# The last expert's rows go to their tokens by one-hot fp32 products, the other experts' rows are summed during its down products

## The chip, the core and the metric

The kernel runs on one core of one Trainium2 chip, alone. The metric is the device time of one execution in microseconds (us), the smaller the better. TensorE does the matrix products (PE in the rows, PEld its weight loads), VectorE (DVE) and ScalarE (ACT) the elementwise work and the reading of PSUM, GpSimd (POOL) some elementwise work and all indirect DMAs, SyncE (SP) issues the large weight loads.

## The reference, cut to what matters

Two layers (DEPTH = 2), each an attention part and then a mixture of experts. SEQ = 512 tokens, D_MODEL = 1024, 16 experts of hidden width 512; every token goes to two of them. All in fp32.

```python
for l in range(DEPTH):
    h = rms_norm(x, norm1_g[l])
    proj = h @ w_in[l]                      # split among three attention groups
    mem_kv = rms_norm(mem, mem_norm_g[l]) @ w_mem_kv[l]
    ...
    x = x + concat(y_ret, y_moba, y_mem) @ w_out[l]
    x = x + hier_moe(rms_norm(x, norm2_g[l]), ...)
# hier_moe: combine[token, e] is the router's weight, non-zero for two experts of a token
for e in range(N_EXPERTS):
    hid = silu(t @ w_gate[e]) * (t @ w_up[e])
    out = out + combine[:, e:e + 1] * (hid @ w_down[e])
```

## The kernel before, in words

The program is written per engine, with semaphores between the engines; the order on each engine is the order of the code. `x` (128 partitions, NT = 4 token tiles of 128, 1024 columns) stays in SBUF.

**Weights.** Each weight matrix comes in units of 512 KB into a ring `stage` of NS = 8 places, issued by SP. ScalarE rounds a unit to fp32r (`w_hi`, `more_hi`), VectorE takes the rest (`w_lo`, `more_lo`), and TensorE forms each product in three fp32r passes (lines 1485 to 1487, function `three`). NX = 6 split units can lie ready. Eight further places, `early`, hold units loaded ahead for one turn in the middle of the expert loop; after that turn they lie idle until the next layer.

**Experts.** Tokens are sorted to slots, up to 128 for an expert in a pass; here every layer has one pass. For expert m (1 to 16) TensorE does the gate and up products, `turn_hidden(m)`, which transposes `hid` from VectorE, and `down(m)` into PSUM banks 2 and 3. The engines interleave the down products of m with the gate and up products of m + 1. `turns` runs experts 1 to 14, then a last `step` serves 15 (`hidden(15)` is its first VectorE instruction), and 16 stands alone: `turn_hidden(16)`, `down(16)`.

**Results.** After `down(m)` ScalarE copies both banks to `ysb` (line 928). GpSimd takes the numbers of the rows (line 666) and scatters them by an indirect DMA (line 669) to `pair_rows` in DRAM, 1024 rows of 4 KB, one for each of a token's two choices. At the end of a pass the three engines `meet`; GpSimd then clears the semaphores and lets all go. `load_results` waits for all scatters and issues eight loads of 512 KB (line 578) to `act`, `proj3` and `hd`. `combine` on VectorE (line 1005) adds each of them, times its weight `wtok`, to a tile of `x`: two for a tile.

**What follows.** After layer 0 layer 1 begins: TensorE transposes `mem_rows` (line 1517), which GpSimd has loaded (line 560), forms the memory projection, and between its parts transposes tile k of `x` (`turn_in(k)`) as `combine` frees it; `turn_in(3)` comes after the first half of unit 4. After layer 1 SP stores the four tiles of `x` (line 553). During the attention part SP waits for places of the ring most of the time.

Of the kernel before, what the change touches and what calls it, by code (L numbers as in the profile page):

```python
# [64 lines left out]
def build(nc, a, out):  # L65
# [4 lines left out]
    with ctx:  # L70
# [109 lines left out]
        with ExitStack() as part:  # L180
# [7 lines left out]
            ysb = sb("ysb", [128, 2, D], scope=part)  # L188
        x_hi = [w_hi[:, k, :] for k in range(NW)] + [more_hi[:, k, :] for k in range(NX - NW)]
# [7 lines left out]
        y_rows = [act[:, q, :] for q in range(4)] + \  # L197
            [pq[3][:, 2 * q:2 * q + 2, :].rearrange("p a c -> p (a c)") for q in range(2)] + \
            [hd[:, q, :, :].rearrange("p g c -> p (g c)") for q in (1, 2)]
# [52 lines left out]

        s_first = sem("s_first")
        s_cb = sem("s_cb")
# [74 lines left out]
        s_cmb = sem("s_cmb")  # L329
# [111 lines left out]
        def meet(eng, p):  # L441

            eng.sem_inc(s_arrive, 1)
            eng.wait_ge(s_go, p + 1)
# [3 lines left out]
        def _(sp):  # L448
# [16 lines left out]
            def load_pass(base0, first):  # L465
# [26 lines left out]
                if first:  # L492
                    sp.wait_ge(s_used, base0 + NW)
                    apart(sp)
# [23 lines left out]
            for layer in range(DEPTH):  # L518
# [30 lines left out]
                with sp.Else():  # L549
                    sp.nop()  # L550
            for t in range(NT):
                sp.wait_ge(s_x, 16 * DEPTH + 4 * (t + 1))
# [5 lines left out]
        def _(pool):  # L558
# [12 lines left out]
            def load_results():  # L571

                for t in range(2):
                    pool.wait_ge(s_yst[t], pool.snap(passes, min_val=1, max_val=NT * DEPTH) * 128 + 16 * t)
                apart(pool)
                for q in range(2 * NT):
                    r0 = SEQ * (q % 2) + 128 * (q // 2)
                    pool.dma_start(y_rows[q], y_d[r0:r0 + 128, :]).then_inc(s_yg[q], 16)

            for layer in range(DEPTH):  # L580
# [7 lines left out]
                if layer > 0:  # L588
                    load_results()
# [52 lines left out]
                pool.wait_ge(s_slot, 1)  # L642

                pool.reg_mov(rounds, 1)
                with pool.Fori(0, rounds) as r:
# [16 lines left out]
                    def scatter(i, e2, col):  # L662

                        pool.wait_ge(s_ye, e2 + (i + 2))
                        apart(pool)
                        pool.tensor_copy(pair_now[:, i, :], slot_pair[:, bass.ds(col, 1)]).then_inc(s_pair, 1)  # L666
                        pool.wait_ge(s_pair, e2 + (i + 1))
                        apart(pool)
# [16 lines left out]
                    with pool.Fori(0, E_N // 2 - 1) as pair:  # L685
                        e2 = pool.snap(pair * 2)
                        for i in range(2):
# [6 lines left out]
                            landed(1 - i, p * 128 + pair * 16 + 16)  # L694
# [12 lines left out]
            load_results()  # L707
# [3 lines left out]
        def _(sc):  # L711
# [15 lines left out]
            for layer in range(DEPTH):  # L727
# [14 lines left out]
                for j in range(4):  # L742
                    bank_hi(j, j, mT_hi[:, 4 * (j // 2):4 * (j // 2) + 4, 128 * (j % 2):128 * (j % 2) + 128])
# [13 lines left out]
                sc.wait_ge(s_x, layer * 16 + 16)  # L757
# [138 lines left out]
                with sc.Fori(0, rounds) as r:  # L896
# [85 lines left out]
                    results(E_N, 0, end[0], U_FIRST + U_E + FT)  # L982
                    sc.wait_ge(s_ye, E_N + 1)
                    meet(sc, p2)
# [5 lines left out]
        def _(dv):  # L990
            dv.sem_inc(s_lo, NS)
            dv.wait_ge(s_cols_t, 1)
            dv.tensor_copy(g_cols[:, :, :, :].rearrange("p w l k -> p (w l k)"), bank[7][:, 0:2 * DEPTH * KT])\
# [6 lines left out]

            def combine(loaded, t):

                for q in (2 * t, 2 * t + 1):
                    dv.wait_ge(s_yg[q], loaded)
# [991 lines left out]
```

## Time and profile before

| | us |
|---|---|
| median of 3 runs | 1157.9 |
| lowest and highest | 1153.62 and 1158.63 |
| the profiled execution's own time | 1153.82 |
| its span | 1151.8 |

2.0 us of the profiled execution lie outside its span. Its own time is near the lowest run and 4.1 us below the median. All times of the trace are counted from the start of the span. TensorE, VectorE and ScalarE are busy for 94%, 78% and 63% of it. The granted clock of TensorE is at its higher level, 2.4 GHz (written 1.00), nearly everywhere, and at the lower, 1.2 GHz (0.50), after some waits. Two stretches matter here: the change of layers, about 545 to 595 us, and the end, about 1100 to 1152 us.

### The profile page before, as it was taken

How to read it: one execution, taken by the hardware profiler on the slowest of the kernel's cores; microseconds unless marked ns; L12 is line 12 of the kernel's file. 1: busy time of each engine (PE TensorE's matmuls, PEld its weight loads, DVE VectorE, ACT ScalarE, POOL GpSimd, SP SyncE). 2: the span in 40 equal slices, each digit the busy share in tenths (PEclk: the TensorE clock that was granted, in tenths of full speed). 3: DMA queues.
4: the chain of work that ended last, by engine and by line, in shares of the span. 5: the costliest groups of instructions: out<-in, count | busy, mean ns of one | idle time of the engine just before them, and what ended most of it. 6: DMA issues, size and time to landing. Idle time of an engine off the chain costs nothing.

```text
span 1151.8 us, 18244 instructions
## 1 busy us (share of the span) xinstructions
PE 1087.6 (94%) x5623; PEld 911.6 (79%) x5623; DVE 893.0 (78%) x1339; ACT 729.2 (63%) x1040; POOL 160.8 (14%) x234
## 2 busy tenths in 40 slices
PE   8999999999999999999789999999999999999990
PEld 7887887878888888888678778888878888888880
DVE  5468777557999999999565877682789999999973
ACT  5635434335888888888463553441479888888860
POOL 1100502001011110110400005200011101111011
PEclk9999999998999999999999999999999999999996
DMA  9522211219999879999863221121599996999966
GB/s 363 160 74 73 68 44 65 92 64 337 372 377 385 336 284 389 387 387 358 298 203 112 72 74 56 65 80 49 186 354 374 387 375 243 377 378 393 391 245 229
DMA packets 121361, 275.11 MB, mean 239 GB/s; under 512 B 13233, under 2 KB 13473, under 8 KB 121168
## 3 DMA queue, kind: packets, MB, share of 16 engines
q1 hardware_dynamic: 106976, 240.25, 56.6%
q0 software_dynamic: 14320, 34.09, 8.2%
q8 instruction: 29, 0.48, 0.2%
q14 instruction: 36, 0.29, 0.1%
HBM read 267.41 MB, written 23.07 MB: 252 GB/s over the span
## 4 chain that ended last, share of the span: by engine, by line
PE 78%; DVE 14%; DMA 4%; issue 2%; ACT 1%; POOL 1%; POOLq 0%; DVEq 0%; ACTq 0%
PE bank L1485 21%; PE bank L1487 21%; PE bank L1486 21%; DVE w_lo L430 3%; PE bank L1856 2%; PE bank L1517 2%; PE bank L1712 1%; DMA proj<-in_mem 1%; PE bank L1875 1%; PE bank L1653 1%; PE bank L1647 1%; DMA hd<-pair_rows 1%; DMA xg<-h_scratch,slot_tok 1%; PE bank L1758 1%; DVE x L1005 1%
## 5 line engine op out<-in xcount | busy, mean ns | idle before, releaser
L424 DVE TENSOR_TENSOR w_lo<-stage,w_hi 128x1024 fp32r<-128x1024 f32 x244 | 293.8, 1220 | 8.8 <-ACT w_hi L419 1.5
L419 ACT ACTIVATE w_hi<-stage 128x1024 fp32r<-128x1024 f32 x236 | 246.4, 1059 | 42.4 <-PE bank L1487 42.4
L1485 PE MATMUL bank<-w_hi,hT_hi 128*128 128x512 f32 x384 | 156.4, 407 | 5.0 <-DVE hT_lo L1019 3.7
L1487 PE MATMUL bank<-w_hi,hT_lo 128*128 128x512 f32 x384 | 150.3, 391 | 0.0
L1486 PE MATMUL bank<-w_lo,hT_hi 128*128 128x512 f32 x384 | 149.7, 390 | 0.0
L424 DVE TENSOR_TENSOR more_lo<-stage,more_hi 128x1024 fp32r<-128x1024 f32 x124 | 146.1, 1219 | 2.4 <-ACT more_hi L419 1.4
L419 ACT ACTIVATE more_hi<-stage 128x1024 fp32r<-128x1024 f32 x124 | 127.7, 1061 | 13.4 <-PE bank L1487 13.1
L1485 PE MATMUL bank<-w_hi,xgT_hi 128*128 128x512 f32 x264 | 103.4, 392 | 1.1 <-DVE xgT_lo L1383 1.1
L1487 PE MATMUL bank<-w_hi,xgT_lo 128*128 128x512 f32 x264 | 102.9, 390 | 0.0
L1486 PE MATMUL bank<-w_lo,xgT_hi 128*128 128x512 f32 x264 | 102.7, 389 | 0.0
L1485 PE MATMUL bank<-more_hi,xgT_hi 128*128 128x512 f32 x248 | 101.9, 411 | 0.0
L430 DVE SCALAR_TENSOR_TENSOR w_lo<-stage,g_cols,w_hi 128x512 fp32r<-128x512 f32 x96 | 70.6, 784 | 40.1 <-ACT w_hi L384 38.6
L384 ACT ACTIVATE w_hi<-stage,g_cols 128x512 fp32r<-128x512 f32 x96 | 63.5, 719 | 55.7 <-PE bank L1487 52.4
L1485 PE MATMUL bank<-w_hi,hidT_hi 128*128 128x512 f32 x248 | 97.4, 393 | 0.3
L1487 PE MATMUL bank<-more_hi,xgT_lo 128*128 128x512 f32 x248 | 97.1, 392 | 0.0
L1486 PE MATMUL bank<-more_lo,xgT_hi 128*128 128x512 f32 x248 | 96.7, 390 | 0.0
L1487 PE MATMUL bank<-w_hi,hidT_lo 128*128 128x512 f32 x248 | 96.6, 389 | 0.0
L1486 PE MATMUL bank<-w_lo,hidT_hi 128*128 128x512 f32 x248 | 96.5, 389 | 0.0
L1485 PEld LDWEIGHTS bank<-w_hi,hT_hi 128*128 128x128 f32 x384 | 72.3, 188 | 19.7 <-issue 5.6
L1487 PEld LDWEIGHTS bank<-w_hi,hT_lo 128*128 128x128 f32 x384 | 72.0, 188 | 15.8
L1486 PEld LDWEIGHTS bank<-w_lo,hT_hi 128*128 128x128 f32 x384 | 72.4, 188 | 12.7
L666 POOL COPY pair_now<-slot_pair 128x1 int32 (+1 forms) x32 | 5.8, 182 | 436.8 <-ACT ysb L928 436.8
(268 smaller groups left out, 2032.2 us busy)
## 6 DMA issues: line engine op xcount, KB each, us to landing
stage<-in_w_exp_up SPq DMA_DIRECT2D x124, 512.0 KB
stage<-in_w_exp_gate SPq DMA_DIRECT2D x122, 512.0 KB
stage<-in_w_exp_down SPq DMA_DIRECT2D x122, 512.0 KB
stage<-in_w_in SPq DMA_DIRECT2D x40, 512.0 KB
stage<-in_w_out SPq DMA_DIRECT2D x16, 512.0 KB
stage<-in_w_mem_kv SPq DMA_DIRECT2D x8, 512.0 KB
h_scratch<-act POOLq DMA_DIRECT2D x8, 512.0 KB, 3.0
act<-pair_rows POOLq DMA_DIRECT2D x8, 512.0 KB, 6.1
```

Of the source, the lines that this page charges most:

```text
L384: ins = eng.activation(w_hi[:, n % NW, part_], stage[:, n % NS, part_], ACT.Copy, scale=gain)
L419: eng.activation(x_hi[n % NX], src, ACT.Copy).then_inc(s_hi, 1)
L424: eng.tensor_tensor(x_lo[n % NX], src, x_hi[n % NX].bitcast(f32), ALU.subtract).then_inc(s_lo, 1)
L430: ins = eng.scalar_tensor_tensor(out=w_lo[:, n % NW, part_], in0=stage[:, n % NS, part_], scalar=gain, in1=w_hi[:, n % NW, part_].bitcast( ...
L1005: dv.scalar_tensor_tensor(out=x[:, t, :], in0=y_rows[q], scalar=wtok[:, q % 2, t:t + 1], in1=x[:, t, :], op0=ALU.mult, op1=ALU.add).then_i ...
L1485: pe.matmul(dst, l_hi, r_hi, start=start, stop=False)
L1486: pe.matmul(dst, l_hi, r_lo, start=False, stop=False)
L1487: return pe.matmul(dst, l_lo, r_hi, start=False, stop=stop)
L1517: ins = pe.transpose(bank[b][:, 128 * q:128 * q + 128], src(q), ident)
L1647: ins = pe.matmul(o[:, 256 + 64 * h:320 + 64 * h], probsT[:, j % 2, 256 * g + 128 * k:256 * g + 128 * k + 128], cv[:, k, 64 * h:64 * h + 6 ...
L1653: ins = pe.matmul(o[:, 64 * h:64 * h + 64], probsT[:, j % 2, 128 * k:128 * k + 128], pq[4][:, k, 64 * h:64 * h + 64], start=k == 0, stop=k ...
L1856: ins = pe.transpose(bank[4 + k // 4][:, 128 * (k % 4):128 * (k % 4) + 128], xg[:, i, 128 * k:128 * k + 128], ident)
```

## The change

Of the 16 experts, the results of the first 15 go through `pair_rows` as before. As soon as their scatters have landed GpSimd issues the eight loads, now to `early`, and only then the load of `mem_rows`. VectorE adds them to `x` (`combine(q)`, q = 0 to 7) with weights `w_pair` that leave out the last expert. The result of expert 16 is copied to `own`. TensorE multiplies it by `tok_at`, which has a one where slot and token belong together (128 slots by 512 tokens): eight fp32 products (`direct(t, half)`), each of 128 by 128 by 512, over tiles t and the two halves of the columns. VectorE adds them from PSUM to `x`, times `w_last`. Tiles 0 and 1 use banks 0 to 3, and tiles 2 and 3 the same banks once VectorE has read them. `shares` on VectorE forms the weights and `tok_at` between the loop and `hidden(15)`. Since rows of `pair_rows` that nobody has written are now loaded, SP first fills them by eight DMAs of 512 KB from DRAM to DRAM, behind the loads of `w_in` of layer 0. The number of a scatter's rows is copied before the wait for its result. The transposes of the memory move from banks 0 to 3 to banks 4 to 7.

```diff
-                    landed(1, p * 128 + 8 * E_N)
                     scatter(0, E_N - 2, E_N - 2)
+                    pool.wait_ge(s_yst[1], p * 112 + 8 * E_N)
+                    apart(pool)
+                    pool.wait_ge(s_yst[0], p * 128 + 8 * E_N)
+                    apart(pool)
+                    for q in range(2 * NT):
+                        r0 = SEQ * (q % 2) + 128 * (q // 2)
+                        pool.dma_start(y_rows[q], y_d[r0:r0 + 128, :]).then_inc(s_yg[q], 16)
                     pool.wait_ge(s_xgt, E_N)
                     load_memory()
-                    pool.wait_ge(s_yst[0], p * 128 + 8 * E_N)
-                    scatter(1, E_N - 2, E_N - 1)
...
+                    def shares():
+                        one_last = one_e[:, :, :, E_N - 1]
+                        dv.tensor_tensor(w_own, wtok[:, :, :], one_last, ALU.mult).then_inc(s_share, 1)
+                        dv.tensor_scalar(in_pass, pos[:, :, :], 0.0, None, ALU.is_ge).then_inc(s_share, 1)
+                        dv.wait_ge(s_share, 2)
...
                     turns(dv, turn)
+                    shares()
...
+                    for q in range(6):
+                        combine(q)
                     dv.wait_ge(s_tail_tab, 1)
-                    read_slots(bank[5][:, 0:E_N * VALS], s_tail, s_tail, 1, (s_pair, E_N))
+                    read_slots(bank[5][:, 0:E_N * VALS], s_tail, s_tail, 1, (s_pair, E_N - 1))
                     dv.wait_ge(s_tail, 5)
                     dv.wait_ge(s_htl, E_N)
-                    meet(dv, p2)
+                    arrive(dv)
+                    for q in range(6, 8):
+                        combine(q)
+                    for t in range(NT):
+                        dv.wait_ge(s_direct, p2 * 4 + (t + 1))
+                        apart(dv)
+                        for half in range(2):
+                            v = x[:, t, 512 * half:512 * half + 512]
+                            ins = dv.scalar_tensor_tensor(out=v, in0=bank[LAST_BANK[t][half]][:, :],
+                                                          scalar=w_last[:, t:t + 1], in1=v, op0=ALU.mult, op1=ALU.add)
+                        ins.then_inc(s_xd, 1)
+                    depart(dv, p2)
...
-                    meet(pe, p2)
+                    arrive(pe)
+                    for half in range(2):
+                        pe.wait_ge(s_last_y, p2 * 2 + (half + 1))
+                        apart(pe)
+                        for t in range(2):
+                            ins = direct(t, half)
+                            if half:
+                                ins.then_inc(s_direct, 1)
+                    for t in range(2, NT):
+                        pe.wait_ge(s_xd, p2 * NT + (NT + t - 1))
+                        apart(pe)
+                        direct(t, 0)
+                        direct(t, 1).then_inc(s_direct, 1)
+                    depart(pe, p2)
...
+                if layer == 0:
+                    for q in range(2 * NT):
+                        sp.dma_start(y_d[128 * q:128 * q + 128, :], a["const_pack"][:, 0:D]).then_inc(s_fill, 16)
```

VectorE at the end of a pass, before (banks by number; `mT_lo` is the first instruction of the next layer, `x<-act,wtok,x` and what follows it come later in that layer):

```order
L1426 TENSOR_TENSOR hidT_lo<-bank4,hidT_hi 128x512
...
L1345 TENSOR_TENSOR probs<-slots,pos 128x512 x2
L1351 TENSOR_REDUCE slot_n<-bank5 128x16
L1352 TENSOR_REDUCE slot_n<-bank5 128x16
L1356 TENSOR_SCALAR slot_tok<-slot_n 128x16
L1358 TENSOR_SCALAR slot_pair<-slot_n 128x16
...
L1019 TENSOR_TENSOR mT_lo<-bank0,mT_hi 128x4x128
```

The same place now, with the first and the last of each row of like instructions (six `x<-early` stand ahead of `slot_n`, two behind):

```order
L1435 TENSOR_TENSOR hidT_lo<-bank4,hidT_hi 128x512
...
L1354 TENSOR_TENSOR probs<-slots,pos 128x512 x2
...
L1485 SCALAR_TENSOR_TENSOR x<-early,prod,x 128x1024
...
L1360 TENSOR_REDUCE slot_n<-bank5 128x16
...
L1367 TENSOR_SCALAR slot_pair<-slot_n 128x16
L1485 SCALAR_TENSOR_TENSOR x<-early,prod,x 128x1024
...
L1516 SCALAR_TENSOR_TENSOR x<-bank0,prod,x 128x512
L1516 SCALAR_TENSOR_TENSOR x<-bank1,prod,x 128x512
...
L1030 TENSOR_TENSOR mT_lo<-bank4,mT_hi 128x4x128
```

All of the summing moved ahead of the next layer's first instruction, where it was spread over the first units of that layer.

TensorE at the change of layers, before (`marks` is the slot table of a possible further pass, `con,proj0` the transposes of the memory):

```order
L1487 MATMUL bank3<-more_hi,hidT_lo 128x512
...
L1841 MATMUL bank5<-marks,probs 128x64 x8
...
L1517 MATMUL bank0<-con,proj0 128x128 x4
L1517 MATMUL bank1<-con,proj0 128x128 x4
L1517 MATMUL bank2<-con,proj0 128x128 x4
L1517 MATMUL bank3<-con,proj0 128x128 x4
```

The same place now:

```order
L1895 MATMUL bank5<-marks,probs 128x64 x8
...
L1995 MATMUL bank0<-own,tok_at 128x512
L1995 MATMUL bank2<-own,tok_at 128x512
...
L1995 MATMUL bank1<-own,tok_at 128x512
L1995 MATMUL bank3<-own,tok_at 128x512
...
L1995 MATMUL bank0<-own,tok_at 128x512
L1995 MATMUL bank1<-own,tok_at 128x512
...
L1567 MATMUL bank4<-con,proj0 128x128 x4
```

Eight products were put between the slot table and the memory's transposes, the last four of them behind waits for VectorE.

GpSimd at the end of a pass, before:

```order
L669 DMA pair_rows<-ysb,pair_now 1024x1024
L560 DMA proj0<-in_mem 128x2x1024
L666 COPY pair_now<-slot_pair 128x1
L669 DMA pair_rows<-ysb,pair_now 1024x1024
...
L578 DMA act<-pair_rows 128x1024 x4
L578 DMA proj3<-pair_rows 128x1024 x2
L578 DMA hd<-pair_rows 128x1024 x2
```

The same place now:

```order
L659 COPY tok_now<-slot_tok 128x1
L662 DMA xg<-h2_scratch,tok_now 128x1024
...
L673 COPY pair_now<-slot_pair 128x1
L678 DMA pair_rows<-ysb,pair_now 1024x1024
...
L712 DMA early<-pair_rows 128x1024 x8
L578 DMA proj0<-in_mem 128x2x1024
```

The last scatter is gone, and the eight loads stand ahead of the load of the memory.

## Rows read from the trace of the kernel before

**Rows 1.** The page: busy time of each engine, share of the span.

```profile
PE 1087.6 (94%) x5623; PEld 911.6 (79%) x5623; DVE 893.0 (78%) x1339; ACT 729.2 (63%) x1040; POOL 160.8 (14%) x234
```

**Rows 2.** The chain that ended last, its end: start us, us, what.

```profile
1124.52 1.09 ACT ysb L928 x2
...
1126.81 3.26 DMA pair_rows<-ysb,pair_now
...
1130.67 2.19 POOL act L578 x4
...
1134.38 12.95 DMA hd<-pair_rows
1147.42 1.28 DVE x L1005
```

**Rows 3.** The same chain at the change of layers.

```profile
550.98 11.27 DMA proj<-in_mem
```

**Rows 4.** Timeline, TensorE at the change of layers: start, us, instruction [idle before, releaser].

```profile
563.79 1.94 PE L1517 MATMUL bank<-con,proj 128*128 128x128 f32 x16 [2.98 <-issue]
...
576.12 1.79 PE L1517 MATMUL bank<-con,x 128*128 128x128 f32 x8 [2.57 <-DVEq L1009]
...
591.86 1.17 PE L1517 MATMUL bank<-con,x 128*128 128x128 f32 x8 [3.02 <-DVE hT_lo L1019]
```

**Rows 5.** Timeline, VectorE and TensorE's weight loads around `hidden(15)` of layer 1.

```profile
1098.96 1.22 DVE L424 TENSOR_TENSOR w_lo<-stage,w_hi 128x1024 fp32r<-128x1024 f32 x1
1100.10 0.69 DVE L1422 TENSOR_TENSOR hid<-bank,sil 128x512 f32<-128x512 f32 x1
...
1100.84 0.51 PEld L1875 LDWEIGHTS bank<-con,hid 128*128 128x128 f32 x4
```

**Rows 6.** Timeline, VectorE, small instructions in the routing.

```profile
831.27 0.29 DVE L1311 TENSOR_TENSOR ckT<-slots,mine 128x128 f32<-128x128 f32 x1
...
837.26 0.16 DVE L1398 TENSOR_TENSOR wtok<-td,gw 128x4 f32<-128x4 f32 x1
```

**Rows 7.** Timeline, GpSimd, the scatter of expert 15 in layer 0 and layer 1.

```profile
549.15 1.84 POOL L669 DMA_INDIRECT pair_rows<-ysb,pair_now  x1 [0.88 <-POOL pair_now L666]
...
1113.09 1.81 POOL L669 DMA_INDIRECT pair_rows<-ysb,pair_now  x1 [0.89 <-POOL pair_now L666]
```

**Rows 8.** Windows: us, busy per engine (x), TensorE's granted clock, DMA share, GB/s.

```profile
547.50:550.00 2.50, 2.50 (x13) 2.07 (x12) 1.81 (x2) 2.31 (x3) 1.03 (x2) 1.00 0.58 185
...
560.00:562.50 2.50, 0.81 (x11) 0.43 (x9) 0.59 (x4) 1.08 (x2) 0.18 (x1) 1.00 1.04 408
...
1132.50:1135.00 2.50, 0.00 (x0) 0.00 (x0) 0.81 (x1) 0.00 (x0) 2.45 (x5) 0.50 0.98 374
```

**Rows 9.** GpSimd's queue in 552.5:555, 555:557.5, 1126:1131: packets, MB, share.

```profile
q0 software_dynamic: 3, 0.00, 0.1%
...
q0 software_dynamic: 175, 0.43, 43.3%
...
q0 software_dynamic: 144, 0.31, 15.6%
```

**Rows 10.** Groups: a 128x512 instruction with a scalar and two tensors on VectorE.

```profile
L430 DVE SCALAR_TENSOR_TENSOR w_lo<-stage,g_cols,w_hi 128x512 fp32r<-128x512 f32 x96 | 70.6, 784 | 40.1 <-ACT w_hi L384 38.6 <-DVE x L1005 0.7 <-DVE ssq L1060 0.5
```

**Rows 11.** Timeline, TensorE: 16 fp32 products of 128 columns, two records each.

```profile
830.90 3.82 PE L1806 MATMUL bank<-ckT,act 128*128 128x128 f32 x32
```

**Rows 12.** Windows where the granted clock of TensorE changes, columns as in Rows 8.

```profile
1128.60:1129.40 0.80, 0.00 (x0) 0.00 (x0) 0.00 (x0) 0.00 (x0) 0.00 (x0) 0.94 0.62 251
...
576.00:577.00 1.00, 0.88 (x5) 0.89 (x6) 0.85 (x2) 0.00 (x0) 1.00 (x3) 0.67 1.07 410
...
579.00:580.00 1.00, 1.00 (x4) 0.83 (x3) 1.00 (x2) 0.77 (x2) 0.00 (x0) 0.62 1.04 420
```

**Rows 13.** Timeline, issues of SP in the attention part of layer 0.

```profile
14.22 59.20 SPq L459 DMA_DIRECT2D stage<-in_w_in  x16
91.31 50.49 SPq L459 DMA_DIRECT2D stage<-in_w_out  x8
```

More of the change, by code:

```diff
@@ L188, in build @@
             ysb = sb("ysb", [128, 2, D], scope=part)
+            own = sb("own", [128, D], scope=part)
+            tok_at = sb("tok_at", [128, SEQ], scope=part)
         x_hi = [w_hi[:, k, :] for k in range(NW)] + [more_hi[:, k, :] for k in range(NX - NW)]
@@ L196, in build @@
         g_rows = early[0:2 * DEPTH * KT, 0, 0:128]
-        y_rows = [act[:, q, :] for q in range(4)] + \
-            [pq[3][:, 2 * q:2 * q + 2, :].rearrange("p a c -> p (a c)") for q in range(2)] + \
-            [hd[:, q, :, :].rearrange("p g c -> p (g c)") for q in (1, 2)]
+        y_rows = [early[:, q, :] for q in range(2 * NT)]
+        tiny = prod[:, :, :].rearrange("p t c -> p (t c)")
+        in_pass, w_own, w_pair = (tiny[:, 8 * i:8 * i + 8].rearrange("p (q t) -> p q t", q=2) for i in range(3))
+        w_last = tiny[:, 24:24 + NT]
+        LAST_BANK = ((0, 1), (2, 3), (0, 1), (2, 3))
         xT = [hd[:, 2, :, :].rearrange("p g c -> p (g c)").rearrange("p (k c) -> p k c", k=KT),
@@ L493, in load_pass @@
                     sp.wait_ge(s_used, base0 + NW)
-                    apart(sp)
+                else:
+                    sp.wait_ge(s_xd, sp.snap(passes, min_val=1, max_val=NT * DEPTH) * NT + NT)
+                apart(sp)
                 e = flat[0] + (2 * TURN_E + 1)
@@ L641, in _ @@
                 apart(pool)
-                pool.wait_ge(s_slot, 1)
+                pool.wait_ge(s_slot, 2)
+                if layer == 0:
+                    pool.wait_ge(s_fill, 16 * 2 * NT)
                 pool.reg_mov(rounds, 1)
@@ L756, in _ @@
                     squares(mem_rows[:, t, :], t)
-                sc.wait_ge(s_x, layer * 16 + 16)
+                if layer == 0:
+                    sc.wait_ge(s_x, 16)
+                else:
+                    sc.wait_ge(s_xd, p * NT + NT)
+                apart(sc)
                 for t in range(NT):
@@ L981, in _ @@
                     sc.reg_mov(rounds, rounds_of(sc))
-                    results(E_N, 0, end[0], U_FIRST + U_E + FT)
-                    sc.wait_ge(s_ye, E_N + 1)
-                    meet(sc, p2)
+                    sc.wait_ge(s_ye, E_N)
+                    arrive(sc)
+                    sc.wait_ge(s_used, end[0] + (U_FIRST + U_E + FT + NW))
+                    apart(sc)
+                    for q in range(2):
+                        sc.activation(own[:, 512 * q:512 * q + 512], bank[2 + q][:, :], ACT.Copy).then_inc(s_last_y, 1)
+                    depart(sc, p2)
                     sc.reg_add(loaded, loaded, (U_PASS - NS) * per_unit)
@@ L1045, in _ @@
                 for t in range(NT):
-                    if layer > 0:
-                        combine(layer * 16, t)
-                    else:
+                    if layer == 0:
                         dv.wait_ge(s_xin[t], 16)
@@ L1537, in turn_in @@
                 def turn_in(k):
-                    pe.wait_ge(s_x, layer * 16 + 4 * (k + 1))
+                    if layer == 0:
+                        pe.wait_ge(s_x, 4 * (k + 1))
+                    elif k < 2:
+                        pe.wait_ge(s_xd, p * NT + (NT if k else 1))
+                        apart(pe)
                     for j in (2 * k, 2 * k + 1):
```

82 lines of the change are left out of this document (49 added, 33 removed).

## The prediction, made before the run

> **What bounds the kernel now.** First the page: TensorE is busy for 94% of the span [rows 1], so time moves only where it waits or stands still. Then the chain of waits, read from its end: the copy of the last expert's result at 1124.52, its scatter, eight loads, and the last sum ending at 1148.70, 3.1 us before the end of the span [rows 2]. TensorE has nothing to do in these 27 us. Then the timeline at the change of layers: TensorE starts again at 563.79, when the memory (landed at 562.25 [rows 3]) and the engines' meeting are done. It works while the loads come in, and waits 2.57 us for the first tile of x and 3.02 us at the last one, which it starts to transpose at 591.86 [rows 4]. So before, the loads are bare at the end, but mostly covered at the change of layers. The change must be priced at each place.
>
> **Part 1, `shares`.** Ten VectorE instructions ahead of `hidden(15)`. VectorE runs straight from a w_lo into `hid`, which ends at 1100.79, and TensorE loads it at 1100.84 [rows 5]: no cover. Six tiny ones of 0.16 us, mostly overlapping but with three waits, I take at 0.8 us, the four of 128x128 at 0.21 us from start to start and 0.3 for the last [rows 6]: 1.7 us in all, 1.2 to 2.3 by taking them all overlapped or all end to end. TensorE has no later wait in which to give this back. Cost 1.7 us per layer; all that follows is later by it.
>
> **Part 2, the change of layers.** The scatter of expert 15 was issued at 549.15, 0.88 us after the copy of its row numbers [rows 7]; that copy is now made ahead, so 550.0 with the shift. SP's queue is full of the next layer's first eight units then. In the old trace GpSimd's queue moved nothing until 555 and 0.43 MB by 557.5 [rows 9]; the scatter is 0.3 MB (the last one alone, third row), so it lands some 7.5 us after its issue, at 557.5 (bounds 3.3 us as in the idle machine [rows 2], and 9). 0.6 us later (1130.07 to 1130.67 in rows 2) GpSimd issues the loads. When they end is a matter of bytes: eight units 4.2 MB, scatter 0.3, loads 4.2, with about 1.0 MB moved in the first 5 us (185 GB/s in rows 8) and 408 GB/s after [rows 8]. From 549.2 that is 5 + 7.7 / 0.408 = 23.9 us, and 1.4 us more since the tail runs on one queue at 374 GB/s [rows 8]: the eighth load lands at 574.5, the sixth at 572.7. The memory stands behind them and lands near 577, 15 us later than now.
>
> VectorE then has, from 572.7: sum 5, 1.3 us [rows 2]; the slot numbers, 0.7; sums 6 and 7 with their waits, 2.9; to 577.6. The sum of tile 0 from PSUM is two instructions of 0.78, overlapping to about 1.45 us [rows 10]: 579.1, tile 1 580.5. Sixteen fp32 products of 128 columns take 3.82 us, less 0.2 for the last one's way: 0.226 each [rows 11], so one of 512 columns 0.9 and a tile's pair 1.8 us at the higher clock (at least 0.5 us, if it went at the rate of an fp32r product; twice 1.8 at the lower clock). The products of tiles 0 and 1 run early, from 562 to 566, under the loads. Those of tile 2 start at 579.2. TensorE has then been idle for 13 us; at the end of the run its clock fell 4.5 us after its last product (0.94 in the window to 1129.4, rows 12). So they run at 1.2 GHz and take 3.6 us, to 582.8. The clock fell again at about 576.3 and was back at about 579.2 (0.67 and 0.62, rows 12), 3 us after work began, so tile 3 is back at 1.8 us: 584.6. Only then comes the memory's transpose, 20.8 us later than 563.79.
>
> What comes back: x is complete, so both waits of rows 4 go, 2.57 and 3.02, and the products that ran at the lower clock from 576.3 to 579.2 [rows 12] give 1.5, as TensorE is warm by then: 7.1 us. VectorE has lost eight sums there and keeps up. Change of layers: +20.8 - 7.1 = **+13.7 us**.
>
> **Part 3, the end.** The scatter of expert 15 goes from 1113.09 to 1113.9. Its issue takes 1.8 us instead of the 1.0 of rows 2, so it lands 4.1 us later, and the loads start at 1118.6. Alone, 4.2 MB at 374 GB/s [rows 8] and 1.3 us before the first byte make 12.5 us: the eighth at 1131.1, the sixth at 1129.4. The last down product ends at 1126.2, so the loads are not quite covered. VectorE: sum 5 to 1130.7, slot numbers to 1131.4, sums 6 and 7 to 1134.3, tile 0 to 1135.7, tile 1 to 1137.1. TensorE's last early product ended at 1130.5, so by 1135.8 it is at the lower clock: tile 2 to 1139.1, its sum to 1140.5; tile 3 to 1140.9, its sum to 1142.4. The last store takes 3.1 us as now: 1145.5 against 1151.8, **-6.3 us**.
>
> **Part 4, the rest.** The fill is 4.2 MB each way on SP's queue. SP issues the last w_in load at 73.4 and then waits until 91.31 for a place of the ring [rows 13]; the work that hides it is TensorE's on units already there. Eight issues of 0.5 us fit, and 4.2 MB take 10.3 us at the 408 GB/s of [rows 8]; they would still fit at 233. Cost 0, and at most a few us if not, but w_out is not multiplied until much later. The wait for the second slot table: 0.1 us a layer. The other banks for the memory: the same splits gate the same products, 0.
>
> **Sum.** 13.7 - 6.3 + 0.2 = +7.6 us, 1161.4 beside the profiled execution's own 1153.8. That execution is 4.1 us below the median, so for the median 1157.9 + 7.6 = **1165.5**. Its own bounds: `shares` -1 to +1.2 in both layers, the products at the higher clock -1.8 at each place, the scatter landing early or late -2 to +1.5: 1159 to 1171.
>
> A rule speaks for the change. The Trainium skill, "DMA: Bandwidth & Descriptors", Rules for kernel authors, says to issue a DMA early, do compute, and wait on it late. Its section "Issuing engines are not separate DMA queues" speaks against it: all queues end in the same 16 engines. By the first alone the eight loads would cost nothing, which is rival A. By the second they only change places with the memory's load and the weights, and the trace agrees: the DMA share is 1.04 in 560 to 562.5 [rows 8].
>
> **Rivals.**
> A, faster: the loads have landed when the last down product ends. For it: the end of the run has free DMA engines. Against it: the bytes above, which must be moved at three times the rate of rows 8 at the end. Then the chain is copy 0.6, three products 2.7, and four tiles at the pace of VectorE with two waits for TensorE, 6.8: the last sum at 1136.3, the end at 1139.4, -12.4 us. At the change of layers the memory's transpose is at 570.9, +7.1, and 7.1 comes back: 0. Time 1157.9 - 12.4 = 1145.5. It decides from the point where the sixth load lands before about 1126.
> B, no change: `shares` is hidden (-3.4) and the clock is never lost in the two gaps (-3.6). Time 1158.5. For it: the small instructions overlap, and the fall of the clock varies (4.5 us at one place, 2.8 at the other). Against it: rows 5.
> C, slower still: the clock stays low, since TensorE gets only two products between two waits; then tile 3 costs 1.8 more at both places and the restart 1.5 to 2. Time 1165.5 + 5.3 = 1171.
>
> **How the numbers follow.** Forecast 0.58 (1160 to 1170), A 0.12, B 0.17, C 0.13. A measurement of this kernel can tell 0.5% from no change, 5.8 us: slower means over 1163.7, faster under 1152.1. Two thirds of the forecast and C lie above: 0.52. The rest of the forecast and nearly all of B is the same: 0.34. A and a little of B: 0.14. The range 1152 to 1173 leaves out A and little else. The likeliest sign's own range is 1160 to 1171.
>
> **What would show it.** In the new profile: a stop of 1.7 us of TensorE before `turn_hidden(15)` in both layers; TensorE idle from about 566 to 579, ended by VectorE's sum of tile 0; the memory landing near 577, its transposes near 585, and no wait for x after them. At the end, in old times (the new ones are 13.9 us later): the last down product ending near 1126, the sixth load landing near 1129, the store of the last tile ending near 1145.5, so a span of 1159.4. The forecast is wrong if the loads land before the last down product, if the memory's transposes start before 575, or if TensorE does not stop at `hidden(15)`.

## The result and the profile after

The changed kernel took 1165.7 us (median of 9 runs, 1162.4 to 1167.8), the kernel before 1158.6 in the same comparison: 1.0079 times as long, with a 95% interval from 1.0062 to 1.0097. The ratio makes it 9.1 us (7.2 to 11.2); between the medians it is 7.1. One of the nine executions of the kernel before took 6209.7 us; without it its median is 1158.3. The forecast was +7.6 and 1165.5. The profiled execution of the changed kernel took 1164.7 us with a span of 1162.5, 10.7 more than the span before.

To see where they lie, both spans are cut at the start of VectorE's `hid`, once for each expert. From expert 1 to 14 every kernel here takes 230.8 to 231.0 us, from 15 to 16 it takes 15.7 to 15.8. The rest, in us, for all kernels of this study ("last add" is the end of VectorE's last instruction on `x`; the stores behind it take 3.1 to 4.2):

| kernel | start to hid 1 | hid 14 to 15, layer 0 / 1 | hid 16 to hid 1 of layer 1 | hid 16 to last add | span | ratio to before [95%] |
|---|---|---|---|---|---|---|
| before | 287.5 | 17.7 / 17.7 | 299.6 | 32.8 | 1151.8 | |
| changed | 286.2 | 19.3 / 19.3 | 314.7 | 26.9 | 1162.5 | 1.0079 [1.0062, 1.0097] |
| e1 new tail behind layer 1 only | 286.7 | 17.7 / 19.3 | 299.2 | 26.6 | 1145.7 | 0.9964 [0.9946, 0.9982] |
| e2 new tail behind layer 0 only | 286.4 | 19.3 / 17.7 | 311.9 | 32.0 | 1163.7 | 1.0119 [1.0093, 1.0144] |
| e3 shares behind hidden_lo(16) | 287.8 | 17.7 / 17.7 | 315.3 | 28.7 | 1164.6 | 1.0082 [1.0057, 1.0106] |
| e4 idle products, 52 and 20 | 288.1 | 19.3 / 19.3 | 314.9 | 26.4 | 1164.3 | 1.0056 [1.0034, 1.0078] |
| e5 shares in the waits of 16 | 288.0 | 17.7 / 17.7 | 313.9 | 27.4 | 1161.7 | 1.0048 [1.0030, 1.0066] |
| e6 idle products, 63 and 28 | 288.5 | 19.3 / 19.3 | 311.4 | 24.6 | 1159.4 | 1.0042 [1.0028, 1.0056] |
| e7 eight banks | 286.8 | 19.3 / 19.3 | 311.5 | 23.4 | 1156.5 | 1.0017 [1.0001, 1.0033] |
| e8 best | 288.9 | 17.7 / 17.7 | 301.2 | 22.6 | 1144.5 | 0.9921 [0.9902, 0.9940] |
| e9 order of the sums | 288.1 | 19.3 / 19.3 | 311.5 | 26.0 | 1161.4 | 1.0064 [1.0040, 1.0088] |
| e10 best, behind both layers | 287.5 | 17.7 / 17.7 | 309.9 | 22.3 | 1151.9 | 0.9972 [0.9957, 0.9986] |
| e11 fill twice | 287.8 | 19.3 / 19.3 | 311.5 | 26.7 | 1162.1 | 1.0092 [1.0058, 1.0127] |

Changed less before: -1.3 (start), +1.6, +15.1, +1.5, -5.9. The columns with hid 16 hold the two places of the forecast. The start and the long segment vary by 2 to 3 us between executions of kernels that do the same in them, so only larger differences, and the short segments, are read from single profiles.

The page of the changed kernel, first line (before: [rows 1]):

```profile
PE 1105.8 (95%) x5655; PEld 918.7 (79%) x5655; DVE 907.2 (78%) x1375; ACT 729.3 (63%) x1040; POOL 185.4 (16%) x230
```

The timeline of VectorE ahead of hidden(15) of layer 1 (before: [rows 5]): `shares` from 1115.31 to 1116.87.

```profile
1114.17 1.22 DVE L434 TENSOR_TENSOR w_lo<-stage,w_hi 128x1024 fp32r<-128x1024 f32 x1
1115.31 0.16 DVE L1464 TENSOR_TENSOR prod<-wtok,one_e 128x8 f32<-128x8 f32 x1
...
1115.95 0.89 DVE L1474 SCALAR_TENSOR_TENSOR tok_at<-slots,slot_n 128x128 f32<-128x128 f32 x4
1116.87 0.69 DVE L1431 TENSOR_TENSOR hid<-bank,sil 128x512 f32<-128x512 f32 x1
```

TensorE there: it stands still for 1.26 us, until `hid`. No such wait stood in the trace before.

```profile
1117.62 0.66 PE L1929 MATMUL bank<-con,hid 128*128 128x128 f32 x4 [1.26 <-DVE hid L1431]
```

The chain of waits at the change of layers (start us, us, what; before: [rows 3]): the scatter of expert 15, the first load, eight sums on VectorE, the direct products of tiles 2 and 3, the transposes of the memory.

```profile
548.90 8.73 DMA pair_rows<-ysb,pair_now
...
558.23 5.74 DMA early<-pair_rows
...
564.13 1.30 DVE x L1485
...
575.72 1.29 DVE x L1485
...
578.89 5.75 PE bank L1995 x8
584.64 0.45 PE bank L1567 x4
```

VectorE's timeline in it. Only the first sum waits for a load: the eight loads land every 1.2 us, from 563.97 to 572.59. The sums follow each other every 1.54 us, though each takes 1.28, since each waits for the sum before it; the slot numbers stand between the sixth and the seventh. The last load has lain ready for 3.1 us when its sum starts. Then VectorE waits 2.73 us for the products of tile 2.

```profile
564.13 1.28 DVE L1485 SCALAR_TENSOR_TENSOR x<-early,prod,x 128x1024 f32<-128x1024 f32 x1 [7.48 <-DMA early<-pair_rows]
565.70 1.28 DVE L1485 SCALAR_TENSOR_TENSOR x<-early,prod,x 128x1024 f32<-128x1024 f32 x1 [0.28 <-DVE x L1485]
...
582.80 1.41 DVE L1516 SCALAR_TENSOR_TENSOR x<-bank,prod,x 128x512 f32<-128x512 f32 x2 [2.73 <-PE bank L1995]
```

TensorE there (before: [rows 4]). Its first product of layer 1 stands at 588.43, and eight products from 589.97 on, of which the first is shown, last 0.6 instead of 0.4 us: the lower clock once more.

```profile
561.54 3.67 PE L1995 MATMUL bank<-own,tok_at 128*128 128x512 f32 x8 [0.62 <-ACT own L1003]
578.89 5.75 PE L1995 MATMUL bank<-own,tok_at 128*128 128x512 f32 x8 [13.68 <-DVE x L1516]
584.48 1.91 PE L1567 MATMUL bank<-con,proj 128*128 128x128 f32 x16
588.43 0.50 PE L1535 MATMUL bank<-w_hi,mT_hi 128*128 128x512 f32 x1 [2.04 <-DVE w_lo L440]
...
589.97 0.63 PE L1535 MATMUL bank<-w_hi,mT_hi 128*128 128x512 f32 x1
```

The chain at the end of the run (before: [rows 2]): again scatter, first load, sums, products of tiles 2 and 3.

```profile
1129.44 3.20 DMA pair_rows<-ysb,pair_now
...
1133.23 3.83 DMA early<-pair_rows
...
1137.22 1.30 DVE x L1485
...
1148.80 1.30 DVE x L1485
...
1151.98 5.93 PE bank L1995 x8
```

### The profile page after: what moved, and what is told of

Same layout as the page of the kernel before. It is cut to its first block, busy times and chain, and to the rows that moved or that the text cites. A ratio compares the mean times of both kernels' runs of the same rounds, so it can differ in the third digit from the quotient of the medians.

```text
span 1162.5 us, 18438 instructions
## 1 busy us (share of the span) xinstructions
PE 1105.8 (95%) x5655; PEld 918.7 (79%) x5655; DVE 907.2 (78%) x1375; ACT 729.3 (63%) x1040; POOL 185.4 (16%) x230
## 4 chain that ended last, share of the span: by engine, by line
PE 78%; DVE 14%; DMA 3%; issue 3%; ACT 1%; DVEq 0%; POOLq 0%; POOL 0%; SPq 0%; ACTq 0%
PE bank L1535 21%; PE bank L1537 20%; PE bank L1536 20%; PE bank L1910 2%; PE bank L1567 2%; DVE w_lo L440 2%; DVE x L1485 2%; PE bank L1766 1%; PE bank L1929 1%; PE bank L1707 1%; PE bank L1701 1%; DMA pair_rows<-ysb,pair_now 1%; PE bank L1995 1%; PE bank L1812 1%; PE bank L1860 1%
## 5 line engine op out<-in xcount | busy, mean ns | idle before, releaser
L1535 PEld LDWEIGHTS bank<-w_hi,hT_hi 128*128 128x128 f32 x384 | 72.3, 188 | 19.3 <-issue 5.6
L678 POOL DMA_INDIRECT pair_rows<-ysb,pair_now x30 | 30.6, 1019 | 345.1 <-ACT ysb L944 181.3
L1537 PEld LDWEIGHTS bank<-w_hi,hT_lo 128*128 128x128 f32 x384 | 72.1, 188 | 15.8
```

Source lines behind the costliest of these rows:

```text
L678: pool.indirect_dma_start(out=y_d, out_offset=bass.IndirectOffsetOnAxis(ap=pair_now[:, i, :], axis=0), in_=ysb[:, i, :], in_offset=None, b ...
L1535: pe.matmul(dst, l_hi, r_hi, start=start, stop=False)
L1537: return pe.matmul(dst, l_lo, r_hi, start=False, stop=stop)
```

## The experiments

The kernels e1, e2, e7, e8, e9 and e10 come from one source in which `TAIL` says for each layer whether its pass ends in the new way. Their line numbers differ from those of the changed kernel.

**e1 and e2: one place at a time.** In e1 layer 0 has written all of `pair_rows`, so that no fill is needed.

```diff
+TAIL = (False, True)
...
+                    if TAIL[layer]:
+                        for q in SUMS[:6]:
+                            combine(q)
...
+                    elif after_old(layer):
+                        combine_old(16 * sum(not t_ for t_ in TAIL[:layer]), t)
```

> The new tail only behind layer 1; layer 0 ends and layer 1 begins as in the kernel before, and there is no fill (layer 0 has written every row of pair_rows). Forecast's reasons (the change of layers costs some 14 us, the end gives some 6 back): kernel before - 6.0 (from the end of the last down product to the end of the span, 21.3 in the changed kernel against 27.3) + 1.3 (the stop at hidden(15) of layer 1) = 1153.9, from 1151 to 1156. Rival, that the end gives nothing by itself and the difference of the two profiles there is chance or drift: 1158 to 1161. Rival A, that both places pay: under 1150.

Measured: 0.9964, 4.2 us less than the kernel before (1154.5 in that comparison), as expected (4.7 less). The long segment is back at 299.2, and the end is 6.3 us shorter than before.

```diff
-TAIL = (False, True)
+TAIL = (True, False)
```

> The new tail only behind layer 0, with the fill; layer 1 ends as in the kernel before. Forecast's reasons: kernel before + 13.7 to 14.7 for the change of layers with its shares, so 1172 to 1173.5. Rival, the change of layers costs only what the medians differ by (7 us) and the end gives nothing: 1166. If e1 and e2 are both right, their two differences to the kernel before add up to the +7.1 us of the changed kernel within 1.5 us.

Measured: 1.0119, 13.7 us more, the lower end of what was expected. The two differences add up to +9.6 us, against +9.1 of the changed kernel by its ratio. By the medians the sum is +10.4 (-3.3 and +13.7), 3.3 over the +7.1 of the changed kernel, where the expectation allows 1.5: the ratios bear the sum out, the medians do not. The result is the sum of two opposite effects, each of which is there without the other. The rival that the end gives nothing is out.

**e3 and e5: where shares stands.**

```diff
                     turns(dv, turn)
-                    shares()
...
                     hidden_lo(E_N)
+                    shares()
```

> The changed kernel with shares moved behind hidden_lo(16), where VectorE waits for the loads anyway. Forecast's reasons (no cover at hidden(15)): the stop of TensorE, 1.26 us in both layers, goes, so 1165.7 - 2.5 = 1163.2, and shares costs nothing at its new place since it ends before the first sum. Rival B: the stop is hidden by other waits, 1165.7 as before.

Measured: 1.0082, nothing gained. The stop is gone (17.7 us from hid 14 to hid 15 in both layers), but at the end the cost is back: 28.7 us from hid 16 to the last add instead of 26.9. VectorE's timeline in e3 shows why. The first sum starts right behind the small instructions and waits for no load; in the changed kernel VectorE came to it 4.6 us behind hid 16 (1132.59 to 1137.22), here 6.4 us.

```profile
1131.94 0.69 DVE L1431 TENSOR_TENSOR hid<-bank,sil 128x512 f32<-128x512 f32 x1 [0.69 <-ACT sil L937]
...
1135.26 0.89 DVE L1474 SCALAR_TENSOR_TENSOR tok_at<-slots,slot_n 128x128 f32<-128x128 f32 x4
...
1138.38 1.28 DVE L1485 SCALAR_TENSOR_TENSOR x<-early,prod,x 128x1024 f32<-128x1024 f32 x1
```

So the expectation that shares costs nothing there was wrong for the end.

```diff
+                    shares()
                     hidden(E_N, 0)
+                    own_tokens()
                     hidden_lo(E_N)
```

> The changed kernel with shares cut in two: the six tiny instructions ahead of hidden(16), where VectorE waited 0.70 us for sil, and the four for tok_at between hidden(16) and hidden_lo(16), where it waited 1.38 us. Theory after the run with shares behind hidden_lo(16): the stop at hidden(15) is real (1.6 us from hid 14 to hid 15), but behind hidden_lo(16) VectorE is the engine that is waited for at the end, so shares cost there what it saved. Here both are avoided: hid 14 to hid 15 back to 17.7 us in both layers, hid 15 to hid 16 unchanged at 15.7 to 15.8, hid 16 to the end of the span unchanged at 29.5 to 29.9; 3.1 us less than the changed kernel, a ratio to the kernel before of 1.0052. Rival: at 1.0079, as the changed kernel, since the attention part varies by more than this.

Measured: 1.0048, 3.6 us less than 1.0079 by the ratios (their intervals overlap a little). The stop is gone in both layers and hid 15 to 16 is unchanged, as expected. The last segment is 27.4, not 26.9: with VectorE ready at the same distance behind hid 16, one sum now waits 0.57 us for its load. To the end of the span it is 31.1, where 29.5 to 29.9 were expected, since the stores took 3.7 instead of 3.1 us. Neither need come from the edit: the third load lands 8.0 us behind hid 16 here and 7.2 to 8.2 in the other kernels with this order of loads, and the stores take 3.1 us in the changed kernel and 4.2 in e11, which does the same there. The profile shows 3.1 us won at hidden(15); what the change of layers keeps of it can't be read from one profile.

```profile
1138.74 1.29 DVE L1487 SCALAR_TENSOR_TENSOR x<-early,prod,x 128x1024 f32<-128x1024 f32 x1 [0.57 <-DMA early<-pair_rows]
```

**e4 and e6: is it the clock?** Products of a constant with itself keep TensorE busy between the early and the late direct products.

```diff
                                 ins.then_inc(s_direct, 1)
+                    idle_work(6, (52, 20)[layer])
                     for t in range(2, NT):
```

> The changed kernel with idle products on TensorE (52 in layer 0, 20 in layer 1, of 128 columns, into a bank not in use) between the first four direct products and the wait for VectorE, so that the clock stays at its higher level. If the clock is what the forecast says it is, tile 2's pair takes about 1.9 instead of 3.9 us at both places and the first products of layer 1 run at the higher level: 2.0 + 2.0 + 1.7 = 5.7 us less, 1160. Rival: VectorE's pace sets both places, so that only part of it is won, 1163; or the granted clock stays low all the same, 1165.7.

Measured: 1.0056. Of the 5.7 us hardly half came, and the profile shows that the clock was not kept. TensorE's timeline, then the granted clock (columns as in [rows 8]):

```profile
566.95 11.77 PE L1573 MATMUL bank<-con 128*128 128x128 f32 x104
581.17 5.24 PE L1995 MATMUL bank<-own,tok_at 128*128 128x512 f32 x8 [2.45 <-DVE x L1516]
```

```profile
580.00:580.50 0.50, 0.00 (x0) 0.00 (x0) 0.50 (x2) 0.00 (x0) 0.50 (x2) 1.00 0.83 49
580.50:581.00 0.50, 0.00 (x0) 0.00 (x0) 0.50 (x2) 0.00 (x0) 0.50 (x2) 0.93 1.46 58
...
584.00:584.50 0.50, 0.50 (x2) 0.20 (x1) 0.00 (x0) 0.00 (x0) 0.00 (x0) 0.66 0.00 0
```

The idle products end at 578.72, and the clock falls 2.2 us later, just ahead of the real ones. It is back 3 us after these began. The test was repeated without the gap:

```diff
-                    idle_work(6, (52, 20)[layer])
+                    idle_work(6, (63, 28)[layer])
```

> As the run with idle products on TensorE, but 63 and 28 of them, so that they end within 0.5 us of VectorE's release instead of 2.45 and 1.87 us before. In that run the clock still fell, 2.2 us after the last idle product, and the pair of tile 2 took 3.7 us. Theory: without the gap the pair takes 1.9 us at the higher clock at both places, the sums of tiles 2 and 3 follow VectorE's pace, and hid 16 to the end of the span is 27.8 to 28.3 us (29.9 in the changed kernel), hid 16 to the memory's transposes 30.3 to 30.8 (32.4). Rival: the clock falls all the same, 29.5 and 32.3.

Measured: 1.0042; 30.8 us from hid 16 to the memory's transposes (32.4 in the changed kernel), 27.7 to the end (29.9). The first is as expected, the second 0.1 us under it, and the four late products now take the 3.67 us of the early ones:

```profile
567.42 14.23 PE L1573 MATMUL bank<-con 128*128 128x128 f32 x126
581.71 3.67 PE L1995 MATMUL bank<-own,tok_at 128*128 128x512 f32 x8
```

So the lower clock costs 1.6 us at the one place and 2.2 at the other (24.6 against 26.9 to the last add), about the 3.6 in all that the forecast had. The first figure is the less certain: the distance from hid 16 to the transposes is 31.8 in e2, which does the same there, since the first load landed 10.9 us behind hid 16 in e2, 11.9 in the changed kernel and 12.3 in e6. Counted from that landing to the transposes it is 20.5 to 21.0 us in the changed kernel, e2 and e11, and 18.4 in e6, so 2.1 to 2.5.

**e7: no second round in the banks.**

```diff
-        LAST_BANK = ((0, 1), (2, 3), (0, 1), (2, 3))
+        LAST_BANK = ((0, 1), (2, 3), (4, 6), (7, 5))
...
+                    early_t = NT if BANKS8 else 2
...
-                        for t in range(2):
+                            for t in range(early_t):
...
+                                if BANKS8 and half and t == NT - 1:
+                                    pe.wait_ge(s_tail, 3)
```

> The changed kernel with the eight direct products in eight banks (0 to 3, 4 and 6, 7 and 5), so that TensorE makes all of them early and VectorE adds eight halves in a row; the memory's transposes go to banks 0 to 3 as soon as tiles 0 and 1 are added. The stops of VectorE for the pairs of tiles 2 and 3 were 2.7 and 0.6 to 0.8 us at both places. Theory (the chain is VectorE's alone from the first load's landing on): hid 16 to the end 29.9 - 3.5 = 26.4; the memory's transposes 3 to 4 us earlier, but the first product of layer 1 waits for VectorE, so 3 us there: 6 to 7 us less than the changed kernel, a ratio to the kernel before of 1.002 to 1.003. Rival: the transposes at the lower clock and the memory's landing (575) take the gain of the change of layers back, 1.005.

Measured: 1.0017, 7.2 us less than the changed kernel by the ratios. The end is 3.5 us shorter, and VectorE adds eight halves in a row:

```profile
1148.02 5.36 DVE L1621 SCALAR_TENSOR_TENSOR x<-bank,prod,x 128x512 f32<-128x512 f32 x8 [0.34 <-DVE x L1575]
```

At the change of layers the memory's transposes stand 3.2 us nearer to hid 16. They take 3.65 us at the lower clock instead of 1.91, as the rival says, but do not undo the gain.

**e9: what sets the stretch of the sums?**

```diff
-SUMS = list(range(8))
-APART_TILES = False
+SUMS = [0, 2, 4, 6, 1, 3, 5, 7]
+APART_TILES = True
...
+                        if APART_TILES and i >= 4:
+                            dv.wait_ge(s_cmb, p2 * 8 + (i - 3))
```

> The changed kernel with the eight loads and sums in the order 0, 2, 4, 6, 1, 3, 5, 7, so that neighbouring sums are of different tiles and none waits for the one before it (0.26 us each). It asks which engine sets the stretch of the sums. Theory now, after the trace of the changed kernel: from the landing of the first load on VectorE sets it, since the sums stand 1.54 us apart though each takes 1.28 and hardly one waits for a load; then the stretch shrinks by up to 7 times 0.26, 1.8 us, at both places: hid 16 to the memory's transposes 30.6 (32.42 in the changed kernel), hid 16 to the end 28.1 (29.91), ratio to the kernel before 1.005. Rival, the forecast's own reading, that the landing of the sixth load (572.7, by bytes) sets it: 32.4 and 29.9, ratio 1.008.

Measured: 1.0064, between the two, though its interval holds both. From hid 16 to the last add it is 0.9 us less, not 1.8, and to the transposes 31.1 us, not 30.6. To the end of the span it is 30.2, which taken alone is the rival's 29.9; but 1.1 us of that are the stores, which took 4.2 us as in e11. Without their own waits the sums catch up with the loads:

```profile
1139.50 2.50 DVE L1575 SCALAR_TENSOR_TENSOR x<-early,prod,x 128x1024 f32<-128x1024 f32 x2 [1.19 <-DMA early<-pair_rows]
```

The landings tell why only half came. In the changed kernel VectorE takes a load every 1.54 us and they land every 1.2 to 1.3 (but 1.8 between the second and the third at the end), so the sixth lies ready for 1.8 us at the change of layers and 1.0 at the end, the eighth for 3.1 and 2.4: VectorE alone sets the stretch. In e9 a sum follows the last after 1.2 to 1.5 us where its load is there, and each of the first six starts within 0.4 us of the landing of its load. A gap in the landings, 2.4 us between the third and the fourth load at the change of layers and 2.5 between the second and the third at the end, then makes VectorE wait 1.1 and 1.2 us. Where the gap comes from stays open. Neither theory is right alone; taking away one limit shows the other.

How much of the 1.54 us is the wait itself? The kernel before has the same wait between the two sums of a tile, and there the second starts 1.31 us after the first. In the changed kernel two semaphore instructions (function `apart`) stand behind the wait, each about 0.11 us; in the kernel before, where one stands between the tiles, it is 1.44. Neighbouring sums of e10, where neither such a wait nor a load holds them up, are 1.22 us apart. So of the 0.32 us between 1.22 and 1.54 the bare wait costs 0.09 and the two instructions behind it the rest. The lines are of the kernel before (two sums with the bare wait) and of e10 (six sums without a wait for each other; two of them wait for their loads). No run takes the two instructions away.

```profile
576.16 2.61 DVE L1005 SCALAR_TENSOR_TENSOR x<-act,wtok,x 128x1024 f32<-128x1024 f32 x2 [0.15 <-DVE x L1005]
...
564.69 7.75 DVE L1575 SCALAR_TENSOR_TENSOR x<-early,prod,x 128x1024 f32<-128x1024 f32 x6 [8.08 <-DMA early<-pair_rows]
```

**e8 and e10: the parts put together.** e8 is e1 with e5's place for shares, e7's banks and e9's order.

```diff
+TAIL = (False, True)
+SHARES_MID = True
+BANKS8 = True
+FILLS = 0
+SUMS = [0, 2, 4, 6, 1, 3, 5, 7]
+APART_TILES = True
```

> The change of layers as in the kernel before and no fill; the new tail behind layer 1 alone, with shares in the waits of expert 16, eight banks, and the loads and sums in the order 0, 2, 4, 6, 1, 3, 5, 7, so that no sum waits for the one before it. From the run with the new tail behind layer 1 alone (4.2 us less than the kernel before): 1.6 less for shares, 3.5 for the stops of tiles 2 and 3, 1 to 2 for the waits between sums (0.26 us each, less what the loads, landing 1.4 us apart, take back): 10.5 to 11.5 us less than the kernel before, a ratio of 0.990 to 0.991. Rival: the loads become the bound and only shares and half of the rest is won, 0.993.

Measured: 0.9921, with medians of 1147.0 us against 1156.7 for the kernel before: 9 to 10 us faster, faster than both kernels, and between the expectation and its rival. VectorE waits 1.29 us for the third load, which lands 2.6 us behind the second (the others mostly 1.2 to 1.3 us apart, not the 1.4 of the expectation), and its adds from PSUM start at 1136.08, 0.6 us behind the last direct product (1128.32 to 1135.43):

```profile
1127.12 2.55 DVE L1575 SCALAR_TENSOR_TENSOR x<-early,prod,x 128x1024 f32<-128x1024 f32 x2 [1.29 <-DMA early<-pair_rows]
...
1136.08 5.35 DVE L1621 SCALAR_TENSOR_TENSOR x<-bank,prod,x 128x512 f32<-128x512 f32 x8
```

```diff
-TAIL = (False, True)
+TAIL = (True, True)
-FILLS = 0
+FILLS = 1
```

> The best kernel so far, but with the new tail behind both layers, and the fill. It asks whether the change of layers can be brought down to what it was. From segments: the changed kernel took 314.7 us from hid 16 of layer 0 to hid 1 of layer 1, the kernel with eight banks 311.5, the kernel before 299.6. With the sums 2 us shorter: 309.5, so still 10 us more than before; at the end of the run as in the best kernel (25.7 from hid 16 to the end, 10.2 less). Sum: a ratio to the kernel before of 1.000 (0.998 to 1.002). Rival: with the stops gone the change of layers costs under 4 us, 0.995.

Measured: 0.9972, just under the expected range, with 309.9 us in the long segment as expected (309.5): with VectorE's stops gone the change of layers still costs some 10 us more than before.

**e11: the fill.**

```diff
                         sp.dma_start(y_d[128 * q:128 * q + 128, :], a["const_pack"][:, 0:D]).then_inc(s_fill, 16)
+                        sp.dma_start(z_d[128 * q:128 * q + 128, :], a["const_pack"][:, 0:D]).then_inc(s_fill, 16)
```

> The changed kernel with the fill made twice (the second 4.2 MB to rows that nobody reads), GpSimd waiting for both. Forecast's step: one fill costs nothing, since SP has 18 us between its last load of w_in and the next free place of the ring, and 8 issues and 10.3 us of transfer fit. Twice 10.3 us is 2.6 us more than that gap, w_out is not needed until later: the time from the start to hid 1 of layer 0 stays within the 286.2 to 288.9 seen so far, and the ratio to the kernel before at 1.008. Rival, that the fill takes DMA time from the weights: 5 us or more for the second fill, ratio over 1.012.

Measured: 1.0092 [1.0058, 1.0127], 287.8 us to hid 1. A second fill keeps the DMA engines busy until about 105 us (DMA share 1.01 and 0.91 in the two windows, 0.34 and 0.02 in the changed kernel), and the segment stays within what it was with one fill and with none (e1: 286.7, e8: 288.9). The ratio alone does not decide: its interval reaches over the rival's 1.012. The segment does, to a microsecond or two; 5 us are ruled out.

```profile
95.00:100.00 5.00, 4.36 (x20) 3.38 (x19) 4.68 (x11) 3.76 (x6) 0.00 (x0) 1.00 1.01 323
100.00:105.00 5.00, 4.30 (x28) 3.58 (x27) 4.64 (x9) 1.73 (x4) 0.00 (x0) 1.00 0.91 299
```

## Why the prediction was right, point by point

**The total.** The places and signs were right, and the sum was some 2 us too low: the ratio says +9.1 us, e1 and e2 together +9.6, the profiled span grew by 10.7 (to 1162.5, forecast 1159.4), where the forecast had +7.6. That the two medians differ by 7.1, within 0.5 us of the forecast, is luck.

**Part 1, shares: right.** 1.7 us of stop in each layer were forecast; TensorE waits 1.26 us, and hid 14 to 15 grew by 1.6 in both. It had no cover, and it had none behind hidden_lo(16) of the last layer either (e3). Rival B's first half is out.

**Part 2, the change of layers: right in its shape, short by up to 3 us.** Without shares the forecast was 12.0 us for the long segment. It grew by 15.1 in the changed kernel, but by 12.3 in e2 and 11.9 in e11, which do the same there. The steps, in us of the run, forecast and measured (hid 16 stands at 551.95 before and 552.06 after, so times compare directly; the forecast had it 1.7 later):

| step | forecast | measured |
|---|---|---|
| scatter landed | 557.5 | 557.63 |
| sum 5 starts | 572.7 | 571.87 |
| sum 7 ended | 577.6 | 577.0 |
| products of tile 2 | 579.2 to 582.8 | 578.89 to 582.80 |
| products of tile 3 end | 584.6 | 584.64 |
| sixth load landed | 572.7 | 570.11 |
| memory landed | 577 | 575.07 |
| memory's transposes | 584.6 | 584.48 |

They agree better than the working deserves, for two errors of 1.7 us cancel. The forecast put hid 16 at 553.7, since the shares delay it, but up to hid 1 this execution was 1.3 us faster. And counted from hid 16 the scatter landed 1.7 us later than forecast: it took 8.7 us from issue, not 7.5, and its issue came 0.5 us later. That is the 1.5 us by which the memory's transposes, 32.4 us behind hid 16, missed the forecast's 30.9.

The reason given for sum 5, that by bytes the sixth load lands at 572.7, isn't what ended its wait: the sixth load landed at 570.11, and sum 5 waited for sum 4, since sums stand 1.54 us apart. Up to one of these 2.6 us is a slip in the working: two loads of 0.5 MB at its 374 or 408 GB/s take 2.6 to 2.8 us, and it put the sixth only 1.8 us ahead of the eighth; the trace has them 2.5 apart. So this step was right in its time and wrong in its cause.

What comes back was forecast as 7.1; from the transposes to hid 1 the changed kernel took 282.3 against 287.7, so 5.4. The step "TensorE is warm by then" failed in this execution: TensorE's clock was low for 3.4 us from 589.9 on (granted clock 0.91 in 589.5 to 590, 0.68 in 593 to 593.5). It was not so in every kernel. Of those whose transposes ran at the higher clock, e3 and e4 also had such slow products, and took 281.9 and 282.6; e2, e5, e6, e9 and e11 had none, and took 279.1 to 280.6, so 7.1 to 8.6 came back. A piece of rival C was there, at some 2 us, in three of these eight kernels; it makes up most of the spread in the long segment.

**Part 3, the end: right in sign, 2 us too hopeful.** Without shares the forecast was -8.0, measured -5.9 to the last add (e1: -6.3). The loads were issued 0.6 us behind hid 16 (1132.59 to 1133.23), forecast 1.0; the forecast gave the scatter 4.1 us with an issue of 1.8, and it took 3.2 with an issue of 1.0. Mis-sized were three terms behind them. The eight sums and the slot numbers ended 17.5 us behind hid 16, forecast 16.7 (1117.6 to 1134.3), by the time between sums. The pair of tile 2 took 3.9 us at the lower clock, forecast 3.3. And tile 3's was put at 1.8 us, but ended 2.2 us behind tile 2's. In all that is 1.8 of the 2.1 us; the rest is small gaps.

**Part 4, the fill: right,** as far as e11 can tell.

**The rivals.** A is out at the change of layers. At the end the first three loads had landed before the last down product ended (about 1141.2; the third landed at 1140.15), but not the sixth, on which it turned: it landed at 1143.91. And the loads were hardly waited for: even with every one in place VectorE, at its own pace of 1.54 us, needs some 17 us behind hid 16 (an estimate: 4.4 us until it is free, 12.9 from the first sum to the end of the last). Of the two rules cited from the Trainium skill, "issue early, wait late" alone would have given A; what the traces bear out is the other, that queues share their engines. The scatter of expert 15 took 8.7 us from issue to landing behind SP's eight units, and 3.2 in the idle machine. B is out by the table, e4 and e6: hid 14 to 15 grew, and the lost clock costs what it was said to.

## What to carry to other kernels

What pays on a bare tail need not pay where the same work was already covered: the same edit gave 6 us at the end of the run and cost 12 to 15 at the change of layers, where the sums had been spread under products. Ask at each place which engine is waited for, and apply the edit only where it pays (e1, e8). When a chain is timed by the landing of transfers, also add up the engine that takes them in, with its waits for itself and the semaphore instructions behind them; here that engine, not the transfers, set the time, and an edit that made it faster gained only half before the transfers did.

## What the runs showed of the hardware

- From start to start, fp32 sums of 128x1024 on VectorE stand 1.22 us apart without a wait for the one before (e10), 1.31 with it alone, 1.44 with one semaphore instruction behind the wait (kernel before) and 1.54 with two (changed kernel).
- TensorE's clock fell 2.2 us after the last of 52 idle products in e4, but some 4 us after the early direct products of the changed kernel, which end at 565.2: in the window from there the granted clock is 0.94, so about 0.6 us of it were at 0.50. A gap of 2.45 us was enough to lose it, and at the end of the run one of 1.87 us (0.87 in 1154.0 to 1154.5, 0.50 behind).

```profile
565.00:570.00 5.00, 0.21 (x1) 0.00 (x0) 4.20 (x4) 0.00 (x0) 0.00 (x0) 0.94 1.03 420
```

- The issue of an indirect scatter on GpSimd took 1.8 us for expert 15 in the kernel before [rows 7] and 1.0 us in the changed one. The copy of its row numbers, which stood right ahead of it, is not the reason: with the same copy 0.9 us ahead 29 of the 32 scatters before took 1.0 us, that of expert 16 among them. The three that took 1.8 to 2.1 us are those that started while VectorE was in the first of two `more_lo` of 128x1024, which it reads from two tensors in SBUF, and they ended 0.9 us behind that instruction. In the changed kernel the scatter starts 0.1 us ahead of it. That VectorE holds the issue up is argued from this; no run tests it. The lines are of the kernel before (VectorE, then GpSimd's scatter of expert 16) and of the changed kernel:

```profile
548.90 2.36 DVE L424 TENSOR_TENSOR more_lo<-stage,more_hi 128x1024 fp32r<-128x1024 f32 x2 [0.69 <-ACT more_hi L419]
...
562.89 1.01 POOL L669 DMA_INDIRECT pair_rows<-ysb,pair_now  x1 [0.87 <-DVEq L443]
...
548.90 0.99 POOL L678 DMA_INDIRECT pair_rows<-ysb,pair_now  x1 [17.96 <-ACT ysb L944]
```
